# Attention blocks of a two-layer kernel: a piece of the next block's scores among the output products, and row sums of squares on ScalarE

## What is computed

```python
def one_block(qblk):
    s = jnp.einsum('bqhmd,bkhmd->bhmqk', qblk, k) * ATTN_SCALE
    p = jax.nn.softmax(s, axis=-1)
    a = p[:, :, 0] - lam * p[:, :, 1]
    return jnp.einsum('bhqk,bkhv->bqhv', a, v)
...
ao = (rms_norm(attn_o, subln_g) * (1.0 - lam_init)).reshape(b, n, ATT_WIDTH)
```

## Time and profile before

| | us |
|---|---|
| median of 3 runs (lowest, highest) | 2924.26 (2922.89, 2927.34) |
| the profiled execution, its own time | 2922.57 |
| its span, first to last instruction | 2920.8 |
| PE busy | 2830.9 (97%) |
| DVE busy | 1433.0 (49%) |
| ACT busy | 902.6 (31%) |
| POOL busy | 636.9 (22%) |
| 60 exponentials, line 677 | 79.6 |
| 640 output passes, line 1820 | 76.8 |
| 32 probT copies, line 685 | 39.6 |
| mean granted TensorE clock | 0.993 |

### The profile page before, as it was taken

How to read it: one execution, slowest core, us unless ns; L and a number is a source line. 1 busy time by engine, 2 the same in 40 slices (tenths; PEclk the granted TensorE clock), 3 DMA queues, 4 the chain that set the end, 5 groups by cost and what they waited for, 6 DMA issues and landing times.

```text
span 2920.8 us, 34652 instructions
## 1 busy us (share of the span) xinstructions
PE 2830.9 (97%) x14282; PEld 2354.6 (81%) x14282; DVE 1433.0 (49%) x1522; ACT 902.6 (31%) x1020; POOL 636.9 (22%) x348
## 2 busy tenths in 40 slices
PE   7999998899999999999999999999999999999997
PEld 4878777887788888788888888888877888888886
DVE  6478128877422226545555565555765213131236
ACT  4332226653211113444442222222333112121122
POOL 0111115214222214222221111111032121222222
PEclk9999999999999999999999999999999999999999
DMA  7111440023111113111111111111021111111123
GB/s 232 63 30 43 147 141 1 1 73 94 44 51 51 46 49 87 51 44 46 49 54 37 37 34 33 37 37 37 23 80 51 51 51 44 51 51 51 44 56 110
DMA packets 276868, 168.52 MB, mean 58 GB/s; under 512 B 5616, under 2 KB 270192, under 8 KB 276336
## 3 DMA queue, kind: packets, MB, share of 16 engines
q1 hardware_dynamic: 275280, 162.88, 18.9%
q10 hardware_dynamic: 1440, 3.51, 0.3%
HBM read 162.17 MB, written 4.19 MB: 57 GB/s over the span
## 4 chain that ended last, share of the span: by engine, by line
issue 52%; PE 36%; POOL 7%; DVE 2%; ACT 2%; DVEq 1%; POOLq 0%; ACTq 0%
PE PS L1485 10%; PE PS L1487 10%; PE PS L1486 10%; POOL Wlo L403 7%; ACT exp L677 1%; DVE acol L1155 1%; PE PS L1656 1%; DVEq L1159 1%; PE PS L1793 1%; PE PS L1577 1%; PE PS L1665 0%; PE PS L1796 0%; PE PS L1646 0%; PE PS L1676 0%; PE PS L1675 0%
## 5 line engine op out<-in xcount | busy, mean ns | idle before, releaser
L403 POOL TENSOR_TENSOR Wlo<-Wraw,Whi 128x1024 fp32r<-128x1024 f32 (+1 forms) x240 | 572.4, 2385 | 2112.8 <-ACT Whi L475 2112.8
L1485 PE MATMUL PS<-Bh,Whi 128*128 128x512 f32 x2176 | 859.6, 395 | 9.7 <-DVE Bl L928 5.9
L1487 PE MATMUL PS<-Bh,Wlo 128*128 128x512 f32 x2176 | 848.8, 390 | 0.0
L1486 PE MATMUL PS<-Bl,Whi 128*128 128x512 f32 x2176 | 848.1, 390 | 0.0
L475 ACT ACTIVATE Whi<-Wraw 128x1024 fp32r<-128x1024 f32 (+1 forms) x240 | 250.4, 1043 | 781.6 <-PE PS L1487 779.1
L1485 PEld LDWEIGHTS PS<-Bh,Whi 128*128 128x128 f32 x2176 | 409.5, 188 | 99.9 <-DVE Bl L928 10.5
L1487 PEld LDWEIGHTS PS<-Bh,Wlo 128*128 128x128 f32 x2176 | 409.1, 188 | 86.4
L1486 PEld LDWEIGHTS PS<-Bl,Whi 128*128 128x128 f32 x2176 | 409.7, 188 | 83.0 <-issue 1.0
L1485 PE MATMUL PS<-Hh,Whi 128*128 128x512 f32 x1120 | 445.4, 398 | 9.9 <-POOL Wlo L403 3.6
L1487 PE MATMUL PS<-Hh,Wlo 128*128 128x512 f32 x1120 | 437.3, 390 | 0.0
L1486 PE MATMUL PS<-Hl,Whi 128*128 128x512 f32 x1056 | 412.5, 391 | 0.0
(11 more groups left out here) (323 smaller groups left out, 3053.6 us busy)
## 6 DMA issues: line engine op xcount, KB each, us to landing
Wraw<-in_w_in SPq DMA_DIRECT2D x64, 512.0 KB, 4.0
Wraw<-in_w_down SPq DMA_DIRECT2D x38, 512.0 KB, 3.7
adaV<-in_ada_w SPq DMA_DIRECT2D x16, 1024.0 KB, 5.2
Wraw<-in_odd_w_in SPq DMA_DIRECT2D x32, 512.0 KB, 4.1
Wraw<-in_w_up SPq DMA_DIRECT2D x32, 512.0 KB, 4.1
Wraw<-in_even_w_in SPq DMA_DIRECT2D x24, 512.0 KB, 3.8
adaW<-in_ada_w SPq DMA_DIRECT2D x8, 1024.0 KB, 11.3
Wraw<-in_even_w_out SPq DMA_DIRECT2D x14, 512.0 KB, 3.7
```

Source lines behind the costliest of these rows:

```text
L403: pool.tensor_tensor(Wlo[:, slot, 0:tiles, :], Wraw[:, slot, 0:tiles, :], Whi[:, slot, 0:tiles, :].bitcast(F32), ALU.subtract).then_inc(lo ...
L1485: mm(out, Whi[:, u % 2, k, :], hi[:, k, c], start=(k == 0), stop=False)
L1486: mm(out, Whi[:, u % 2, k, :], lo[:, k, c], start=False, stop=False)
L1487: return mm(out, Wlo[:, u % 2, k, :], hi[:, k, c], start=False, stop=(k == KT - 1))
```

## The change

The first third of map "zero"'s scores (bank 0, 512 keys) of blocks 5 to 31 is taken out of `scores(b)` and put into the block before, between the products of `output(b - 4)`: after the products t = 0 to 6 and ahead of t = 7 to 9. It waits for the first exponential of the block before alone, which has then read banks 0 to 2, instead of both. `scores(b)` keeps three rounds for map "one" and two for map "zero". The maximum of bank 0 moves on VectorE to the end of the step before, behind `combine`.

The squares of the output rows move from GpSimd, and their sums from VectorE, to ScalarE: a second pass over the same PSUM rows with `SQUARE` and an accumulated sum follows the scaled copy, and the semaphore `o_ready` is raised behind it. All semaphores between the squares and the sums go, and the root waits with a drain of ScalarE instead.

```diff
+    EARLY = range(HEADS + 1, BLOCKS)
...
-        def block_square(b):
-
-            pool.wait_ge(sem("o_ready"), b + 1)
-            if b >= 2:
-                pool.wait_ge(sem("o_summed"), b - 1)
-            pool.tensor_tensor(osq[:, b % 2, :], obig[:, b, :], obig[:, b, :], ALU.mult).then_inc(sem("osq_ready"), 1)
-
-        for b in range(HEADS, BLOCKS + 5):
+        for b in range(HEADS, BLOCKS):
             if b < 2 * HEADS:
                 keys_split(b - HEADS)
-            if b < BLOCKS:
-                block_query(b)
-            if b >= 5:
-                block_square(b - 5)
+            block_query(b)
...
-            act.activation(obig[:, b, :], rows_in(b), IDN, scale=acol[:, b % 3, 9:10]).then_inc(sem("o_ready"), 1)
+            act.activation(obig[:, b, :], rows_in(b), IDN, scale=acol[:, b % 3, 9:10])
+            act.activation(osq[:, b % 2, :], rows_in(b), SQUARE, scale=acol[:, b % 3, 9:10],
+                           accum_out=ocol[:, b:b + 1]).then_inc(sem("o_ready"), 1)
...
         def output_root(h):
-            act.wait_ge(sem("o_summed"), 16 * h + 16)
+            act.drain()
...
+        def first_max(b):
+            dve.wait_ge(sem("s0_psum"), 3 * b + 1)
+            dve.reduce_max(acol[:, b % 3, 0:1], bank(0), AX.X)
+
         def shifts(b):
 
             s = b % 3
-            for i in range(2):
-                dve.wait_ge(sem("s0_psum"), 3 * b + i + 1)
-                dve.reduce_max(acol[:, s, i:i + 1], bank(i), AX.X)
+            if b not in EARLY:
+                first_max(b)
+            dve.wait_ge(sem("s0_psum"), 3 * b + 2)
+            dve.reduce_max(acol[:, s, 1:2], bank(1), AX.X)
...
-            if c >= 6:
-                block_sum(c - 6)
+            if c + 1 in EARLY:
+                first_max(c + 1)
...
-            for i, (k1, w1, k0, w0) in enumerate(((0, 256, 0, 512), (256, 512, 512, 512), (768, 512, 1024, 256))):
+            zeros = ((0, 512), (512, 512), (1024, 256))[1 if b in EARLY else 0:]
+            for i, (k1, w1) in enumerate(((0, 256), (256, 512), (768, 512))):
                 for n, (q, k) in enumerate(terms):
                     one = mm(PS[:, S1 + k1:S1 + k1 + w1], q[64:128], k[64:128, k1:k1 + w1], start=(n == 0), stop=(n == end))
-                    if i == 2 and n == 0:
-                        pe.wait_ge(sem("s1_psum"), 3 * b + 1)
-                    zero = mm(PS[:, S0 + k0:S0 + k0 + w0], q[0:64], k[0:64, k0:k0 + w0], start=(n == 0), stop=(n == end))
+                    if i < len(zeros):
+                        k0, w0 = zeros[i]
+                        if k0 == 1024 and n == 0:
+                            pe.wait_ge(sem("s1_psum"), 3 * b + 1)
+                        zero = mm(PS[:, S0 + k0:S0 + k0 + w0], q[0:64], k[0:64, k0:k0 + w0], start=(n == 0), stop=(n == end))
...
+        def early_scores(b):
+
+            terms = split_terms(b)
+            pe.wait_ge(sem("exp_ready"), 2 * b - 1)
+            for n, (q, k) in enumerate(terms):
+                zero = mm(bank(0), q[0:64], k[0:64, 0:512], start=(n == 0), stop=(n == 2))
+            zero.then_inc(sem("s0_psum"), 1)
...
             for t in range(10):
+                if t == 7 and b + 4 in EARLY:
+                    early_scores(b + 4)
                 ins = mm(rows_in(b), probT[:, b % 2, t, :], vT[:, t, h * P:(h + 1) * P], start=(t == 0), stop=(t == 9))
```

More of the change, by code:

```diff
@@ L1175, in combine @@
             stt(weights_of(b, 0)[:, :], weights_of(b, 1)[:, :], acol[:, s, 11:12], weights_of(b, 0)[:, :], ALU.mult, ALU.add).then_inc(sem("weights_ready"), 1)
-        def block_sum(b):
-            dve.wait_ge(sem("osq_ready"), b + 1)
-            dve.tensor_reduce(ocol[:, b:b + 1], osq[:, b % 2, :], AX.X, ALU.add).then_inc(sem("o_summed"), 1)
         for c in range(BLOCKS + 1):
@@ L1218, in dve_program @@
         rows_scaled(1)
-        for b in (27, 28, 29):
-            block_sum(b)
         gated_rows(0)
@@ L1224, in dve_program @@
         rows_scaled(3)
-        block_sum(30)
         gated_rows(2)
-        block_sum(31)
         dve.wait_ge(sem("g7_ready"), 1)
@@ L1784, in scores @@
             else:
-                terms = ((qh[:, s, :], kh[h][:, :]), (ql[:, s, :], kh[h][:, :]), (qh[:, s, :], kl[:, h, :]))
-                pe.wait_ge(sem("ql_ready"), b - HEADS + 1)
-                pe.wait_ge(sem("kl_ready"), min(b - HEADS + 1, HEADS))
+                terms = split_terms(b)
             if b:
@@ L1790, in scores, with split_terms @@
             end = len(terms) - 1
-            for i, (k1, w1, k0, w0) in enumerate(((0, 256, 0, 512), (256, 512, 512, 512), (768, 512, 1024, 256))):
+            zeros = ((0, 512), (512, 512), (1024, 256))[1 if b in EARLY else 0:]
+            for i, (k1, w1) in enumerate(((0, 256), (256, 512), (768, 512))):
                 for n, (q, k) in enumerate(terms):
                     one = mm(PS[:, S1 + k1:S1 + k1 + w1], q[64:128], k[64:128, k1:k1 + w1], start=(n == 0), stop=(n == end))
-                    if i == 2 and n == 0:
-                        pe.wait_ge(sem("s1_psum"), 3 * b + 1)
-                    zero = mm(PS[:, S0 + k0:S0 + k0 + w0], q[0:64], k[0:64, k0:k0 + w0], start=(n == 0), stop=(n == end))
-                one.then_inc(sem("s1_psum"), 1)
-                zero.then_inc(sem("s0_psum"), 1)
+                    if i < len(zeros):
[3 more added lines that the diff above has]
+                        zero = mm(PS[:, S0 + k0:S0 + k0 + w0], q[0:64], k[0:64, k0:k0 + w0], start=(n == 0), stop=(n == end))
+                one.then_inc(sem("s1_psum"), 1)
+                if i < len(zeros):
+                    zero.then_inc(sem("s0_psum"), 1)
+        def split_terms(b):
+            s, h = b % 2, b % HEADS
+            pe.wait_ge(sem("ql_ready"), b - HEADS + 1)
+            pe.wait_ge(sem("kl_ready"), min(b - HEADS + 1, HEADS))
+            return ((qh[:, s, :], kh[h][:, :]), (ql[:, s, :], kh[h][:, :]), (qh[:, s, :], kl[:, h, :]))
+        def early_scores(b):
+            terms = split_terms(b)
+            pe.wait_ge(sem("exp_ready"), 2 * b - 1)
+            for n, (q, k) in enumerate(terms):
+                zero = mm(bank(0), q[0:64], k[0:64, 0:512], start=(n == 0), stop=(n == 2))
+            zero.then_inc(sem("s0_psum"), 1)
         def turn(b):
```

## The result

The changed kernel takes 2939.97 us (median of 4 runs, 2939.16 to 2942.7), the kernel before 2924.05 us on the same chip: a ratio of 1.0054, 95% interval 1.0042 to 1.0066. It is slower by 15.9 us. The forecast was 11.1 us slower, 2935.4 us, with a range up to 2939.0: the sign was right, the time lies 1 us above the range, and the step from before is 4.8 us more than forecast.

The account below looks back on a forecast made before the run. Bound before: the 6.18 us loop of scores, VectorE maxima and ScalarE exponentials. Sum: +0.28, 26 blocks x (6.59 - 6.18) = 10.7, tail -0.28 + 0.44: +11.1 us on 2924.26, forecast 2935.4 us; own range 2931 to 2939, whole 2927 to 2939.

Parts of the forecast that it names:

- the gain of the chain: Scores through VectorE's maxima to ScalarE's exponentials and the next scores: 5.90 us per block, 0.28 less.
- ScalarE's loop: Output end, rows, squares, probT copy, transposes, output passes with the moved products: 6.59 us per block, the longest loop.
- the first rival: Only TensorE's own loop binds, 6.42 us per block, with probT arriving in time: 2931.0 us, chance 0.17.
- the term of the scores: On TensorE, from the first score product to the transposes: 1.91 us for 1.95, hardly shorter.
- What TensorE pays: Part on TensorE's costs per block: scores 1.91, moved products 1.04 and 0.09 into the scores, a loop of 6.42 us.
- Early piece: Three 512-column products moved among the output products: 0.69 us bare plus row changes, 1.04 us per block.
- Entry into the scores: TensorE's change from 128-row output products to 64-row score products, no longer hidden by idle time: 0.09 us per block.
- The tail: After the last block: output 30 waits for rows 29, squares 0.34 us, and the drain ahead of the root 0.1: 0.44.
- The cheap early piece: Changing rows inside the output costs nothing, the moved products cost 0.69 us: about +1.8, 2926.1 us, chance 0.16.
- the pure chain: Only the scores-maxima-exponentials loop counts, 5.90 us per block, moved products fitting TensorE's idle 0.85: -7.1, 2917.2 us, chance 0.05.
- table load: Squares on ScalarE need two table loads of 1.28 us per block: near 2969 us, chance 0.02.
- Strict order of the products: Score products of the two row halves wait for one another: scores 2.16 us, TensorE's loop 6.67, 2937.7 us, chance 0.02.

Follow-up runs that it names:

- the first experiment: Changed kernel with the 256-column product group of map zero, and its wait for `s1_psum`, back in the third round: 2938.54 us, 1.0045 times before.
- both experiments on it: On the kernel with the wait in the third round and squares back: first bank's products cut into two 256-column groups, 2944.56 us; only 256 columns wide, 2922.79 us.
- the last two kernels: Changed kernel with map zero's moved products behind the last output product and its 256-column group in the third round, 2922.14 us; the same with squares and sums back, 2919.86 us.

## Why the prediction was right in sign and short in size

**What bounds after.** Right that the gain of the chain would be more than eaten up, and that TensorE pays for it. That gain itself (forecast 0.28 us) shows only where the chain binds again, with the early piece ahead of the scores: 3.04 + 2.93 = 5.97, a gain of 0.21. Wrong in which loop: the forecast had ScalarE's loop at 6.59 us and TensorE waiting for probT; what was measured is the first rival's mechanism, TensorE's own loop, at 6.72 in place of that rival's 6.42.

**The step that failed** is the term of the scores in "What TensorE pays": 1.91 us from the first score product to the transposes, with the "one" side's products at an unbroken pitch. It measured 2.15. The text counted what the moved products leave behind and did not count where the wait for `s1_psum` comes to stand, though it holds back every instruction behind it on its engine. With the wait back in the third round the term is 1.92 to 1.94 and the period 6.59. The 0.13 us between 6.59 and 6.72, over 26 blocks 3.4 us, are most of the 4.8 us by which the forecast was short. The period of 6.72 is the forecast's 6.42 for TensorE's loop with 0.24 more for the scores and 0.06 for the small excesses below. The rest of the 5.2 us by which the span missed: 0.16 up to block 5, 0.70 in the last block, -0.04 in the tail, and the 1.0 behind it, for which the forecast had nothing and the rows show no cause.

**The other terms.** Early piece 1.04 us: measured 0.99 and 0.06 for the slower restart of the passes, together 1.05. Entry into the scores 0.09: six passes need 0.67 and 0.06 and take 0.86, so 0.13. TensorE's loop without the misplaced wait 6.42: 6.49. ScalarE's loop 6.59: 6.59, with small errors that cancel (its signal to TensorE 0.10 for 0.14, outputs with the early piece and the signal 3.52 for 3.48). The added squares 0.34: 0.36 (536.22 to 536.83 in the first experiment is 0.61 for rows and squares, of which the rows were 0.25). The tail 0.44: 0.40. The split queries, called a block ahead, were 0.17 us late for the first early piece alone. The last block, forecast 0.28 shorter than before, took 0.42 longer: it has the misplaced wait, and VectorE idles 0.44 us in it ahead of a small reduction (636.65 us) with no release in the profile:

```profile
636.65 0.15 DVE L1162 TENSOR_REDUCE acol<-acol 128x1 f32<-128x2 f32 x1 [0.44 <-issue]
```

The same gap stands in the last block of the kernel with the squares alone (623.23 us) and of two others with the squares on ScalarE, but not of the one with the half-wide piece, and of none with the squares back. So it came with moving them and not with the early piece; its cause is open.

**The rivals.** The cheap early piece and the pure chain fell: the early piece costs its columns and the row change, as both experiments on it show. No table load appeared between exponential and square, the squares start 0.27 us after the rows like any other pass. Strict order of the products fell as well, though its numbers (scores 2.16, loop 6.67, 2937.7 us) came nearest to the measured ones: with lopsided rounds and no wait in the way the scores took 1.92 us, and in the changed kernel too a "one" product starts ahead of an earlier "zero" product (531.49 and 531.60). Judged by the total alone, the wrong rival would have won.

## What to carry to other kernels

When a group of instructions is taken out of an interleaved order, look at what its neighbours' waits now stand behind: a wait that cost nothing in the third round costs a stall when it moves up to the second, and it holds the engine's other stream as well. Work that uses half of TensorE's rows belongs beside its like; between full-height products the same three products cost 0.5 us more (6.49 for 5.97), and next to the scores one of them was nearly free. And the idle time of the bounding wait (0.85 us a block) is the whole budget: an edit that spends 1.04 us of the idle engine to take 0.28 off the chain loses even if the chain gives all of that.

## What the runs showed of the hardware

The misplaced wait on TensorE cost more than the time until its release. The product that releases it ends at 531.65 (531.37 and 0.28), 0.07 before the held "one" product would have started (531.72); the weights are loaded only from 531.82, the product starts at 531.83, and it holds its successor for 0.33 us (531.83 to 532.16) instead of 0.23. 0.11 and 0.10 are the 0.21 us between the 2.15 and the 1.94 us of scores.

Two profiles can differ by the clock before the changed blocks begin. The windows view of the run with the squares back and the wait in the third round, against the same stretch of the changed kernel, both with the columns of the earlier trace rows:

```profile
420.00:450.00 30.00, 26.96 (x135) 17.80 (x134) 17.03 (x31) 14.69 (x18) 12.72 (x9) 0.91 0.00 1
```

```profile
420.00:450.00 30.00, 26.74 (x156) 18.94 (x144) 19.91 (x35) 16.66 (x21) 14.09 (x10) 1.00 0.00 1
```

The first blocks, alike in both kernels, ran at a mean of 0.91 once, which is the lower of the clock's two levels (1.2 for 2.4 GHz) for a part of the 30 us, and at 1.00 in the other. TensorE idled up to 2.75 us at a time there in both, waiting for exponentials, so the idling alone does not tell them apart. Between the transposes of blocks 0 and 1 there lie 8.63 us in the one profile (441.20 to 449.83) and 6.41 in the other (439.83 to 446.24). These 2.2 us are as much as lies between the medians of the last two kernels (2922.14 and 2919.86), which is why the periods were read from the traces and not worked out from medians. Whether this is what scatters the times of one kernel is not shown: there is one profile of each.
